# Query columns of the first layer in seven products, sixteen convolution taps and the channel norm moved into attention

## The chip, the core and the metric

One core of one Trainium2 chip runs the whole program in fp32. The metric is the device time of one execution in microseconds, lower is better.

## What is computed

Two layers of a diffusion backbone on 256 context and 256 latent tokens (T = 512, D = 1024). Cut to what matters here, a layer is:

```python
h = rms_norm(x) * (1 + scale) + shift                       # modulated by c
cq, ckv, kr, glu, dq, dk, dv, gates = split(h @ w_in)       # one projection, three branches
a, g = split(glu); u = a * sigmoid(g)                       # 512 channels
u = depthwise_conv(u, conv_w, 31 taps) + conv_b             # along the tokens
o_conv = silu(layer_norm(u, ln_g, ln_b))                    # norm over the 512 channels
o_mla  = attend(q, k, v)                                    # 8 heads, from cq, ckv, kr
o_diff = diff_attend(dq, dk, dv, lam)                       # 4 heads of two maps each
y = sum(sigmoid(gates[b]) * (o_b @ w_o_b) for b in branches)
x = x + g1 * (y @ w_out)
x = x + g2 * moe(rms_norm(x) * ...)                         # 32 experts, two per token
```

Context tokens share all weights and attend to context alone. The second layer keeps only the latent tokens. `dq`, `dk` and `dv` are 512 columns wide.

## The kernel before

The program is written by hand for five engines: TensorE (PE), ACT, DVE, POOL and SP, which only issues DMAs. Each engine has its own function with the instructions in the order in which they run; they meet at semaphores. Weights come in units of up to 2 MB through a ring of three slots (`ring`, loaded by SP in a fixed order: glu0, lora, glu1, dq, ukv, dk, dv, mg0, mg1, mo0, ...). PE's `mm` (L474) writes PSUM banks of two classes: "a" banks are evicted by ACT (through the helper `f`, L1358) and "d" banks by DVE. Every fp32 matmul leaves two records in the trace.

*Projections.* PE computes the GLU columns, the low-rank columns, then `dq`, `ukv` (with `uq`), `dk`, `dv`. `dq` is four output tiles of 128 columns, eight matmuls of 512 tokens each; ACT copies a tile to `qd` and writes its latent half once more with swapped blocks, for the rotary part (`swapped` tells DVE). `dk` and `dv` are already computed in Strassen's form (Winograd's variant): instead of eight products of quarters there are seven, named q, x, r, 11, 12, y, z, each four matmuls of 256 tokens. It needs sums of quarters of the weights, made on DVE: s1 and s2 before the products (`key_sums_ahead`), s4 and s3 in place of weights that the products q and x have read (`key_sums_behind`), sums of quarters of the tokens (`h_sums`), and additions of the results (`key_tiles`).

*Convolution.* The 31 taps of four channel tiles are 124 instructions on DVE, each 128x512: a `scalar_tensor_tensor` through the helper `stt` (L1865) that adds a weighted shift of the input. `conv(n)` writes the next n of them; DVE spreads them between its other work in the projections. When the last is done DVE sets `conv_v`.

*Attention and merge.* Layer 0 then has 32 units (8 heads in blocks) and the units of the differential branch behind them. In unit u PE does `turn(u)` (four or two transposes of probabilities, L857, which wait for `pt_ready` of the unit before and for the probabilities of this one), `scores(u+2)`, the values of the unit before, and some matmuls of the merge (the gate columns, `group_step`, again in seven products, with weight sums on POOL: `sums_ahead`, `sums_behind`; then the branch columns, `branch_step`). DVE does `peak(u+2)` (row maxima, L2288), `probs(u+1)` (L2302, L2303), copies of the values (L2317) and additions of merge tiles (L2411 to L2425). ACT copies the transposed probabilities (`pt_copy(u)`, which sets `pt_ready`) and computes the exponentials.

*Channel norm.* A table of unit numbers says in which unit each step of the norm stands, the same table for all engines (`conv_norm(u)` in each): LN_MEAN (POOL adds the channel tiles, PE sums over the partitions, DVE subtracts the mean, four `stt`), squares on ACT a unit later, LN_VAR (again POOL and PE), CONV_ROOT (reciprocals on DVE), CONV_SCALE (DVE), CONV_TANH (ACT), CONV_OUT (DVE, four `stt` that set `conv_out`).

*What follows `conv_out` in layer 0.* SP loads 1 MB of rows (`silu_load`, L3168, "crow") into the region where the norm kept its squares and its sigmoids, so it waits for all four `conv_out`. ACT has one instruction on these rows, `silu_tanh`, 128x2048, written behind the exponential of unit 22; in ACT's queue the `pt_copy` of unit 23 stands behind it. DVE multiplies the rows in unit 24 and SP loads the first columns of the next modulation after that.

Of the kernel before, what the change touches and what calls it, by code (L numbers as in the profile page):

```python
# [9 lines left out]
KD = D // 128  # L10
# [63 lines left out]
def build(nc, a):  # L74
# [15 lines left out]
    with ctx:  # L90
# [22 lines left out]
        yt = [arena[:, 16384 + T * c:16384 + T * c + T] for c in range(4)] + [yt_more[:, c] for c in range(3)] + [arena[:, 43760:44272]]  # L113
# [165 lines left out]
        AHEAD_SUMS = [("tokens", 0)] + [(w_, "dk") for w_ in ("s1", "s2", "s4_0", "s3_0", "s4_1", "s3_1")] + [(w_, "dv") for w_ in ("s1", "s2", "s4", "s3")]  # L279
        STEPS = [(*w_, 0) for w_ in AHEAD_SUMS] + [("s1", 0, 0), ("s2", 0, 0)]  # L280
# [5 lines left out]
        STEPS += [(*w_, 1) for w_ in AHEAD_SUMS]  # L286
# [151 lines left out]
        def _(pe):  # L438
# [197 lines left out]
            for l in range(DEPTH):  # L636
# [58 lines left out]
                w = grid(unit(("dq", l, 0))[:, 0:4096], KD)  # L695
                for i in range(HD):
                    column_tile("a", ("dq", l, i), lambda k: w[:, k, 128 * i:128 * i + 128], q0, 128, KD, h)
                    if i == 0:
                        ada_finish(("glu", l, 1))
                used(("dq", l, 0), "a")  # L700
                ada_units(("dq", l, 0))
# [16 lines left out]
                w = unit(("dk", l, 0))[:, 0:4096].rearrange("p (k g t m) -> p k g t m", k=KD, g=2, t=2)  # L718
                key_sum = arena[:, 26864:27888].rearrange("p (k g m) -> p k g m", k=4, g=2)
                pe.wait_ge(sums_ready, pool_sums("tokens", 0, l))  # L720
                for g in range(2):
                    w11, w12, w21, w22 = w[:, 0:4, g, 0], w[:, 4:8, g, 0], w[:, 0:4, g, 1], w[:, 4:8, g, 1]
                    for name, cls, cols, toks, needs in (("q", "a", w11, h[:, 0:4, 0:CTX], None), ("x", "a", w21, h_sums[0], "s1"),
                                                         ("r", "d", key_sum[:, :, g], h_sums[1], "s2"), ("11", "d", w12, h[:, 4:8, 0:CTX], None),
                                                         ("12", "d", w11, h[:, 4:8, CTX:T], f"s4_{g}"), ("y", "d", w21, h_sums[2], f"s3_{g}"),
                                                         ("z", "d", w22, h_sums[3], None)):
                        ps = begin(cls, (name, l, "dk", g))
                        if needs:
                            pe.wait_ge(sums_ready, pool_sums(needs, "dk", l))
                        for k in range(4):  # L730
                            last = mm(ps[:, 0:CTX], cols[:, k, :], toks[:, k, :], k == 0, k == 3)
                        end(cls, last)
                used(("dk", l, 0), "d")
                ada_units(("dk", l, 0))
# [618 lines left out]
        def _(act):  # L1353
# [97 lines left out]
            for l in range(DEPTH):  # L1451
# [65 lines left out]
                for i in range(HD):  # L1517
                    ps = take(("dq", l, i))
                    f(qd[:, i, q0:T], ps[:, 0:NQ], ACT.Copy)
                    ins = swap_blocks(PTq[:, i, :], ps[:, CTX - q0:NQ])  # L1520
                    give(ins)
# [1967 lines left out]
```

## Time and profile before

| | |
|---|---|
| three runs, us | 1452.44, 1456.43, 1459.77 (median 1456.43) |
| the profiled execution, us | 1456.56 |
| its span, first to last instruction, us | 1454.6 |
| busy: PE, DVE, ACT, POOL | 1371.5, 802.9, 400.4, 151.6 us |
| mean granted clock of PE | 0.983 of full |

PE is busy for 94% of the span. The 40 slices of the page show DVE at 8 to 9 tenths in the projections (up to about 208 us) and at less in the first attention; POOL is used there for the weight sums. The chain of work that ended last is PE for 74%, with waits for expert weights and for DVE in the later stages. Layer 0's projections run from about 47 to 208 us, its attention from 208 to about 414 us.

### The profile page before, as it was taken

What the parts mean: (1) busy time and instruction counts of PE and PEld (TensorE: products, weight loads), DVE (VectorE), ACT (ScalarE), POOL (GpSimd) and SP (SyncE); (2) the same over time, 40 slices, a digit from 0 to 9 for tenths busy, and PEclk for the clock granted to TensorE, in tenths of its full rate; (3) what the DMA queues carried; (4) which work ended last, traced back from release to release, by engine and by line L of the source; (5) the groups of instructions that cost most, each with busy time, mean ns of one, the idle gap of its engine ahead of it and who ended that gap; (6) DMA issues with size and microseconds to landing.
All of it is one profiled execution on the core that took longest, in us unless ns stands there. A gap on an engine that the chain in (4) does not pass through costs nothing.

```text
span 1454.6 us, 20103 instructions
## 1 busy us (share of the span) xinstructions
PE 1371.5 (94%) x7782; PEld 855.9 (59%) x7782; DVE 802.9 (55%) x1830; ACT 400.4 (28%) x883; POOL 151.6 (10%) x126
## 2 busy tenths in 40 slices
PE   5999999999999999989998869999999999999876
PEld 3444777754444445655555437777678876666543
DVE  2499875778897944523131117996853434344322
ACT  4113634532222012312221224363442203000001
POOL 0020033200011210012212110101000110000000
PEclk9999999999999999989999999999999999999998
DMA  9412230144526446399999968234523489999996
GB/s 379 171 36 79 95 116 11 77 147 171 181 80 227 192 189 274 131 354 418 419 419 420 415 259 342 94 116 144 185 77 145 177 325 378 399 419 420 419 420 239
DMA packets 59553, 347.69 MB, mean 239 GB/s; under 512 B 8388, under 2 KB 15172, under 8 KB 28352
## 3 DMA queue, kind: packets, MB, share of 16 engines
q1 hardware_dynamic: 53856, 335.86, 58.5%
q0 software_dynamic: 5024, 8.40, 1.6%
q10 hardware_dynamic: 576, 2.10, 0.4%
q8 instruction: 65, 1.06, 0.3%
q14 instruction: 32, 0.26, 0.1%
HBM read 343.44 MB, written 11.80 MB: 244 GB/s over the span
## 4 chain that ended last, share of the span: by engine, by line
PE 74%; DVE 8%; SPq 8%; DMA 7%; issue 1%; ACT 1%; DVEq 0%; POOLq 0%; ACTq 0%
PE bank L474 70%; DMA arena<-w_up_in 5%; SPq L3246 4%; DVE arena L1865 4%; SPq L3212 2%; PE bank L857 2%; SPq L3260 2%; DMA arena<-y 1%; PE bank L1232 1%; PE bank L574 1%; ACT arena L1358 1%; DMA x<-x_in 1%; DVE am L2288 0%; PE bank L1252 0%; DVE arena L2393 0%
## 5 line engine op out<-in xcount | busy, mean ns | idle before, releaser
L474 PE MATMUL bank<-arena 128*128 128x256 f32 (+9 forms) x5848 | 1125.7, 428 | 23.9 <-DMA arena<-w_up_in 12.8
L474 PEld LDWEIGHTS bank<-arena 128*128 128x128 f32 (+3 forms) x5848 | 644.3, 161 | 425.4 <-issue 311.4
L1358 ACT ACTIVATE arena<-bank 128x512 f32<-128x512 f32 (+5 forms) x439 | 202.7, 481 | 818.9 <-PE bank L474 718.8
L1865 DVE SCALAR_TENSOR_TENSOR arena<-arena,bank 64x256 f32<-64x256 f32 (+2 forms) x121 | 57.7, 478 | 242.7 <-ACT arena L1358 183.6
L1865 DVE SCALAR_TENSOR_TENSOR arena<-arena,early 128x512 f32<-128x512 f32 (+1 forms) x254 | 138.7, 612 | 0.9
L2288 DVE TENSOR_REDUCE am<-bank 128x1 f32<-128x512 f32 (+1 forms) x96 | 55.4, 598 | 73.9 <-PE bank L474 73.6
L1358 ACT ACTIVATE arena<-bank,am 128x512 f32<-128x512 f32 (+1 forms) x96 | 58.6, 613 | 115.2 <-DVE am L2291 115.0
L3030 POOL TENSOR_TENSOR arena<-arena 128x512 f32<-128x512 f32 (+1 forms) x32 | 37.3, 1167 | 369.4 <-DVE arena L1865 369.4
L1358 ACT ACTIVATE arena<-arena 32x256 f32<-32x256 f32 (+5 forms) x99 | 48.2, 516 | 15.3 <-DVE arena L2317 9.9
L3069 POOL DMA_INDIRECT y<-arena,routing x33 | 32.9, 997 | 180.7 <-ACT arena L1358 180.7
L474 PE MATMUL bank<-down_last,arena 128*128 128x256 f32 (+2 forms) x192 | 46.8, 469 | 1.0 <-DVE arena L2723 0.6
L857 PEld LDWEIGHTS bank<-con,arena 128*128 128x128 f32 x240 | 29.9, 141 | 25.4 <-issue 12.3
L857 PE MATMUL bank<-con,arena 128*128 128x128 f32 x240 | 38.6, 275 | 4.6 <-DVE arena L2303 4.6
L474 PE MATMUL bank<-down_more,arena 128*128 128x256 f32 (+2 forms) x160 | 41.1, 510 | 1.0 <-DVE arena L2723 1.0
L2390 DVE SCALAR_TENSOR_TENSOR arena<-arena 128x1024 f32<-128x1024 f32 x28 | 34.1, 1217 | 5.9 <-DMA arena<-adaT_in 5.9
L474 PEld LDWEIGHTS bank<-down_last,arena 128*128 128x128 f32 (+2 forms) x192 | 28.2, 170 | 10.4 <-issue 6.2
L2393 DVE SCALAR_TENSOR_TENSOR arena<-arena 128x1024 f32<-128x1024 f32 x28 | 34.1, 1219 | 0.0
L474 PE MATMUL bank<-con 128*128 128x128 f32 x178 | 24.4, 292 | 10.0 <-DVE x L1948 10.0
L1358 ACT ACTIVATE arena<-x 128x1024 f32<-128x1024 f32 x14 | 14.8, 1056 | 67.8 <-DVE x L2552 47.0
L574 PE MATMUL bank<-con,arena 128*128 128x128 f32 x112 | 16.5, 299 | 16.2 <-ACT arena L1358 16.2
L2550 DVE TENSOR_TENSOR arena<-bank,arena 128x512 f32<-128x512 f32 x12 | 8.3, 692 | 40.0 <-PE bank L474 40.0
L2860 DVE COPY arena<-bank 128x128 f32<-128x128 f32 x33 | 9.6, 291 | 36.6 <-PE bank L1252 36.2
(262 smaller groups left out, 992.9 us busy)
## 6 DMA issues: line engine op xcount, KB each, us to landing
arena<-w_gate_in SPq DMA_DIRECT2D x60, 1024.0 KB, 22.1
arena<-w_up_in SPq DMA_DIRECT2D x60, 1024.0 KB, 24.4
arena<-w_down_in SPq DMA_DIRECT2D x45, 1024.0 KB, 20.7
arena<-mg_in SPq DMA_DIRECT2D x12, 2048.0 KB, 8.1
arena<-adaT_in SPq DMA_DIRECT2D x40, 512.0 KB, 3.6
arena<-adaT_in SPq DMA_DIRECT2D x16, 1024.0 KB, 7.0
arena<-ada_in SPq DMA_DIRECT2D x6, 2048.0 KB, 15.7
arena<-mo_in SPq DMA_DIRECT2D x6, 2048.0 KB, 8.4
```

The source lines that it names most:

```text
L474: return nc.tensor.matmul(out, w, rhs, start=start, stop=stop)
L574: last = nc.tensor.transpose(ps[:, 128 * k:128 * k + 128], src[:, 512 * half + 128 * k:512 * half + 128 * k + 128], ident)
L857: last = nc.tensor.transpose(PS[6][:, kt * 128:kt * 128 + 128], src[:, kt * 128:kt * 128 + 128], ident)
L1358: return nc.scalar.activation(out, in_, fn, **kw)
L1865: return V.scalar_tensor_tensor(out, in0, sc, in1, op0=op0, op1=op1)
L2288: ins = V.reduce_max(am[:, c + m:c + m + 1], PS[b][:, 0:nk], AX.X)
L2390: V.scalar_tensor_tensor(column_product, w, 1.0, grid(silu_at[l][:, 0, :], m), op0=MUL, op1=MUL, accum_out=ada[l][:, c_, 0:1]).then_inc(dv ...
L2393: V.scalar_tensor_tensor(w, w, 1.0, grid(silu_at[l][:, 1 - l, :], m), op0=MUL, op1=MUL, accum_out=ada[l][:, c_, 1 - l:2 - l]).then_inc(dve ...
L3030: G.tensor_tensor(yt[c][:, q0:T], yt[c][:, q0:T], gt8[:, c, q0:T], op=ADD).then_inc(s[done], 1)
L3069: pool.indirect_dma_start(out=yd[l][:, :], out_offset=bass.IndirectOffsetOnAxis(ap=to, axis=0), in_=yy[0:64 + C, p, :], in_offset=None, bo ...
L3212: sp.dma_start(to[..., 512 * q:512 * q + 512], src[..., 512 * q:512 * q + 512]) \
L3246: sp.dma_start(to, src).then_inc(gu_ready[j], 16)
```

## The change

Four things, cut to their core.

1. In layer 0 `dq` is computed in the seven products too: 14 products of four matmuls of 256 tokens in place of 4 x 8 matmuls of 512. The code of `dk` becomes `paired_columns(of)` and serves both. DVE gets the weight sums and result sums of `dq`; ACT copies q and x and writes the swapped blocks from SBUF when a group of tiles is complete.
2. Sixteen taps of layer 0 (two in each of units 0 to 7) leave the projections for attention, and the norm's steps stand later.
3. The merge's intermediate tiles `yt` change places, so that the tiles written first don't lie on the input of the late taps; POOL adds the norm's channels later in its order.
4. In layer 1 some taps change places with the key additions, one or two positions.

```diff
-        yt = [arena[:, 16384 + T * c:16384 + T * c + T] for c in range(4)] + [yt_more[:, c] for c in range(3)] + [arena[:, 43760:44272]]
+        yt = [yt_more[:, c] for c in range(3)] + [arena[:, 43760:44272]] + [arena[:, 16384 + T * c:16384 + T * c + T] for c in range(4)]
...
+        PAIRED = (("dq", "dk"), ("dk",))
...
-        LN_MEAN, LN_VAR = (3, 2), (8, 7)
-        CONV_ROOT = ({9 + c: (c,) for c in FOUR}, {8: (0,)})
-        CONV_SCALE = ({13 + c: (c,) for c in FOUR}, {8: FOUR})
-        CONV_TANH = ({15 + c: (c,) for c in FOUR}, {10: FOUR})
-        CONV_OUT = ({17 + c: (c,) for c in FOUR}, {12: FOUR})
+        LATE_TAPS = (2,) * 8
+        LN_MEAN, LN_VAR = (10, 2), (14, 7)
+        CONV_ROOT = ({15: (0, 1), 16: (2, 3)}, {8: (0,)})
+        CONV_SCALE = ({17: (0, 1), 18: (2, 3)}, {8: FOUR})
+        CONV_TANH = ({19: (0, 1), 20: (2, 3)}, {10: FOUR})
+        CONV_OUT = ({21: (0, 1), 22: (2, 3)}, {12: FOUR})
...
+                if l == 0:
+                    paired_columns("dq")
+                    ada_finish(("glu", l, 1))
+                else:
...
+                if l == 0:
+                    for g in range(2):
+                        ps = take(("q", l, "dq", g))
+                        give(f(qd[:, 2 * g, 0:CTX], ps[:, 0:CTX], ACT.Copy))
+                        ps = take(("x", l, "dq", g))
+                        give(f(qd[:, 2 * g + 1, CTX:T], ps[:, 0:CTX], ACT.Copy))
+                    for g in range(2):
+                        act.wait_ge(empty["d"], Dn[("z", l, "dq", g)])
+                        for i in (2 * g, 2 * g + 1):
+                            ins = swap_blocks(PTq[:, i, :], qd[:, i, CTX:T])
+                    ins.then_inc(s["swapped"], 1)
...
-                    if b == 0 and c == 0:
+                    if b == 0 and c == 4:
                         act.wait_ge(s["conv_v"], seen(l, "conv_v", 1))
...
                 conv(12)
+                if l == 0:
+                    pair_sums_ahead("dq")
                 glu_up(3)
...
-                conv(16)
+                if l == 0:
+                    conv(4)
+                    pair_sums_behind("dq", 0)
+                else:
+                    conv(16)
...
+                if l == 0:
+                    pair_tiles("dq", 0, 2)
+                    pair_tiles("dq", 0, 3)
+                    pair_sums_behind("dq", 1)
...
-                conv(len(CONV) - conv_at[0])
...
+                conv(len(CONV) - conv_at[0] - (0 if l else sum(LATE_TAPS)))
...
                 def conv_norm(u):
...
+                    if l == 0 and u < len(LATE_TAPS):
+                        conv(LATE_TAPS[u])
+                        if u == len(LATE_TAPS) - 1:
+                            conv_end()
...
                     sums_behind(0, 0)
                     upper(0, 0)
                     sums_ahead(0, 1)
                     corner(0, 0)
+                    sums_behind(0, 1)
+                    upper(0, 1)
+                    sums_ahead(0, 2)
+                pool.wait_ge(s["conv_v"], seen(l, "conv_v", 1))
+                pool.wait_ge(full["a"], A[("uv", l, 3)])
+                add_channels(cv)
+                if l == 0:
+                    corner(0, 1)
                 pool.wait_ge(s["conv_sq"], seen(l, "conv_sq", CT))
                 add_channels(lora)
```

What the tables of units do to the order is plainer in the order itself. First DVE at the `dq` columns; the last GLU tile is the row whose input is `arena,bank`. Before:

```order
L1865 SCALAR_TENSOR_TENSOR arena<-arena,early 128x512 [waits dve_step] x12
L1865 SCALAR_TENSOR_TENSOR arena<-arena,bank 128x2x256 [waits act_tile_empty,dve_tile_full]
L1865 SCALAR_TENSOR_TENSOR arena<-arena,early 128x512 [waits dve_step,dve_tile_empty]
L1865 SCALAR_TENSOR_TENSOR arena<-arena,early 128x512 [waits dve_step] x3
L2037 TENSOR_SCALAR arena<-arena,early 128x512 x2
L1865 SCALAR_TENSOR_TENSOR arena<-arena,early 128x512 [waits dve_step] x10
L2094 RECIPROCAL arena<-arena 128x512 [waits act_tile_empty]
```

and with the change:

```order
L1889 SCALAR_TENSOR_TENSOR arena<-arena,early 128x512 [waits dve_step] x12
L2162 TENSOR_TENSOR arena<-arena 128x8x128 [waits ring_ready0]
L2163 TENSOR_TENSOR arena<-arena 128x1024 [waits sums_ready]
L1889 SCALAR_TENSOR_TENSOR arena<-arena,bank 128x2x256 [waits act_tile_empty,dve_tile_full,sums_ready]
L1889 SCALAR_TENSOR_TENSOR arena<-arena,early 128x512 [waits dve_step,dve_tile_empty]
L1889 SCALAR_TENSOR_TENSOR arena<-arena,early 128x512 [waits dve_step] x3
L2169 TENSOR_TENSOR arena<-arena 128x4x128 [waits act_tile_full]
L2171 TENSOR_TENSOR arena<-arena 128x4x128 [waits act_tile_full,sums_ready]
L2219 RECIPROCAL arena<-arena 128x512 [waits act_tile_empty,sums_ready]
```

The two sums ahead stand in front of the last GLU tile, and two sums behind stand where twelve taps and bias instructions were.

Next DVE in units 19 to 24, at the last steps of the channel norm; the `stt` that waits `conv_act` is CONV_OUT, the one of 128x2048 is DVE's part on the rows. Before, from unit 19 on:

```order
L1865 SCALAR_TENSOR_TENSOR arena<-arena 128x512 [waits conv_act]
L2288 TENSOR_REDUCE am<-bank 128x1 [waits scores]
L2291 TENSOR_SCALAR am<-am 128x1 [waits dve_step]
L2302 RECIPROCAL am<-am 128x1 [waits exp_ready_0]
L2303 TENSOR_SCALAR arena<-arena,am 128x512 [waits dve_step]
L2317 COPY arena<-bank 128x128 [waits pv_full]
L2411 TENSOR_TENSOR arena<-arena,bank 128x256 [waits act_tile_empty,dve_tile_full]
L1865 SCALAR_TENSOR_TENSOR arena<-arena 128x512 [waits conv_act]
```

and with the change, from the end of unit 21 to the end of unit 22:

```order
L2475 TENSOR_TENSOR arena<-arena,bank 128x256 [waits sums_ready,dve_tile_full]
L1889 SCALAR_TENSOR_TENSOR arena<-arena 128x512 [waits conv_act] x2
L2345 TENSOR_REDUCE am<-bank 128x1 [waits scores]
L2348 TENSOR_SCALAR am<-am 128x1 [waits dve_step]
L2359 RECIPROCAL am<-am 128x1 [waits exp_ready_0]
L2360 TENSOR_SCALAR arena<-arena,am 128x512 [waits dve_step]
L2374 COPY arena<-bank 128x128 [waits pv_full]
L2478 TENSOR_TENSOR arena<-bank,arena 128x256 [waits dve_tile_full]
L1889 SCALAR_TENSOR_TENSOR arena<-arena 128x512 [waits conv_act] x2
```

The last CONV_OUT stood behind the merge tile L2411 in unit 20; now it stands behind the merge tile of L2478 (L2421 before) in unit 22.

Last ACT from the late tanh steps (`arena<-arena,early`) to the rows. With the change:

```order
L1370 ACTIVATE arena<-arena,early 128x512 [waits conv_scaled]
L1370 ACTIVATE arena<-arena 128x512 [waits conv_act]
L1370 ACTIVATE arena<-bank 128x512 [waits pt_full]
L1370 ACTIVATE arena,am<-bank,am 128x512 [waits pt_full,scores_max]
L1370 ACTIVATE arena<-bank 128x512 [waits pv_full,pt_full]
L1370 ACTIVATE arena,am<-bank,am 128x256 [waits pt_full,scores_max]
L1370 ACTIVATE arena<-arena 128x2048 [waits silu_rows_loaded]
L1370 ACTIVATE arena<-bank 128x512 [waits pt_full]
L1370 ACTIVATE arena,am<-bank,am 128x256 [waits pt_full,scores_max]
```

Here the rows' instruction (128x2048) keeps its place behind the exponential of unit 22 and ahead of the copy of unit 23; the norm's steps have moved towards it.

## Rows read from the trace of the kernel before

**Rows 1.** The page: busy time of the engines, share of the span, instructions.

```profile
PE 1371.5 (94%) x7782; PEld 855.9 (59%) x7782; DVE 802.9 (55%) x1830; ACT 400.4 (28%) x883; POOL 151.6 (10%) x126
```

**Rows 2.** Windows: length, busy PE, PEld, DVE, ACT, POOL, clock, DMA share, GB/s.

```profile
114.00:141.00 27.00, 27.00 (x64) 11.98 (x63) 26.69 (x35) 8.38 (x18) 0.00 (x0) 1.00 0.15 64
208.00:250.00 42.00, 40.43 (x216) 30.72 (x218) 21.54 (x65) 19.62 (x47) 16.57 (x15) 1.00 0.14 51
```

**Rows 3.** Timeline of ACT: start, us, instructions, idle before and releaser in brackets.

```profile
121.29 2.14 ACT L1358 ACTIVATE arena<-bank 128x512 f32<-128x512 f32 x5 [5.18 <-PE bank L474]
128.09 2.14 ACT L1358 ACTIVATE arena<-bank 128x512 f32<-128x512 f32 x5 [4.67 <-PE bank L474]
...
160.78 0.38 ACT L1358 ACTIVATE arena<-bank 128x256 f32<-128x256 f32 x1 [0.85 <-PE bank L474]
162.51 0.39 ACT L1358 ACTIVATE arena<-bank 128x256 f32<-128x256 f32 x1 [1.34 <-PE bank L474]
```

**Rows 4.** Timeline of DVE in the projections.

```profile
111.47 0.69 DVE L1865 SCALAR_TENSOR_TENSOR arena<-arena,bank 128x512 f32<-128x512 f32 x1 [4.71 <-PE bank L474]
...
115.77 6.71 DVE L1865 SCALAR_TENSOR_TENSOR arena<-arena,early 128x512 f32<-128x512 f32 x10
...
133.09 1.23 DVE L2191 TENSOR_TENSOR arena<-arena 128x1024 f32<-128x1024 f32 x1
...
160.78 0.69 DVE L2198 TENSOR_TENSOR arena<-arena 128x512 f32<-128x512 f32 x1 [1.02 <-PE bank L474]
...
164.24 0.42 DVE L2127 TENSOR_TENSOR arena<-arena,bank 128x256 f32<-128x256 f32 x1 [0.18 <-PE bank L474]
```

**Rows 5.** Timelines of PE (two turns), DVE (mean) and ACT (squares) in attention.

```profile
252.28 0.38 PE L857 MATMUL bank<-con,arena 128*128 128x128 f32 x2
...
255.15 0.66 PE L857 MATMUL bank<-con,arena 128*128 128x128 f32 x4
...
224.91 2.48 DVE L1865 SCALAR_TENSOR_TENSOR arena<-bank,arena 128x512 f32<-128x512 f32 x4 [0.82 <-PE bank L474]
...
228.89 2.18 ACT L1358 ACTIVATE arena<-arena 128x512 f32<-128x512 f32 x4
```

**Rows 6.** Timelines of DVE, SP, ACT, PE around the rows' load, and its DMA issue.

```profile
285.56 0.69 DVE L1865 SCALAR_TENSOR_TENSOR arena<-arena 128x512 f32<-128x512 f32 x1
...
293.43 0.42 DVE L2421 TENSOR_TENSOR arena<-bank,arena 128x256 f32<-128x256 f32 x1 [1.54 <-PE bank L474]
...
286.27 0.33 SPq L3168 DMA_DIRECT2D arena<-crow_in  x1
...
arena<-crow_in SPq DMA_DIRECT2D x1, 1024.0 KB, 4.6
...
292.52 1.91 ACT L1358 ACTIVATE arena<-arena 128x2048 f32<-128x2048 f32 x1
294.32 0.59 ACT L1358 ACTIVATE arena<-bank 128x512 f32<-128x512 f32 x1
...
295.83 0.38 PE L857 MATMUL bank<-con,arena 128*128 128x128 f32 x2
```

**Rows 7.** Timeline of PE and windows (columns of Rows 2) where the clock was down.

```profile
780.17 6.59 PE L474 MATMUL bank<-arena 128*64 128x256 f32 x32 [1.57 <-DMA arena<-w_up_in]
...
831.90 3.67 PE L474 MATMUL bank<-arena 128*64 128x256 f32 x32
...
873.91 3.78 PE L474 MATMUL bank<-con 128*128 128x128 f32 x16 [10.04 <-DVE x L1948]
...
873.00:874.50 1.50, 0.59 (x3) 0.59 (x3) 1.47 (x2) 0.55 (x1) 0.00 (x0) 0.50 0.97 415
877.50:879.00 1.50, 1.50 (x10) 1.24 (x10) 1.21 (x4) 1.14 (x2) 0.00 (x0) 0.74 1.05 448
```

**Rows 8.** Timelines of DVE and POOL: one `stt` while POOL adds.

```profile
278.04 1.45 DVE L1865 SCALAR_TENSOR_TENSOR arena<-arena 128x512 f32<-128x512 f32 x1
...
277.85 1.09 POOL L2988 TENSOR_TENSOR arena<-arena,routing 128x512 f32<-128x512 f32 x1 [4.35 <-PE bank L474]
```

More of the change, by code:

```diff
@@ L693, in _ @@
                 sums(("loraS", l, 0), [P[:, 0, q0:T]])
[L695 to L701, printed above, removed]
+                key_sum = arena[:, 26864:27888].rearrange("p (k g m) -> p k g m", k=4, g=2)
@@ new lines, in paired_columns @@
+                def paired_columns(of):
+                    w = unit((of, l, 0))[:, 0:4096].rearrange("p (k g t m) -> p k g t m", k=KD, g=2, t=2)
+                    pe.wait_ge(sums_ready, pool_sums("tokens", 0, l))
+                    for g in range(2):
+                        w11, w12, w21, w22 = w[:, 0:4, g, 0], w[:, 4:8, g, 0], w[:, 0:4, g, 1], w[:, 4:8, g, 1]
+                        for name, cls, cols, toks, needs in (("q", "a", w11, h[:, 0:4, 0:CTX], None), ("x", "a", w21, h_sums[0], "s1"),
+                                                             ("r", "d", key_sum[:, :, g], h_sums[1], "s2"), ("11", "d", w12, h[:, 4:8, 0:CTX], None),
+                                                             ("12", "d", w11, h[:, 4:8, CTX:T], f"s4_{g}"), ("y", "d", w21, h_sums[2], f"s3_{g}"),
+                                                             ("z", "d", w22, h_sums[3], None)):
+                            ps = begin(cls, (name, l, of, g))
+                            if needs:
+                                pe.wait_ge(sums_ready, pool_sums(needs, of, l))
+                            for k in range(4):
+                                last = mm(ps[:, 0:CTX], cols[:, k, :], toks[:, k, :], k == 0, k == 3)
+                            end(cls, last)
+                    used((of, l, 0), "d")
+                    ada_units((of, l, 0))
@@ new lines, in _ @@
+                if l == 0:
+                    paired_columns("dq")
+                    ada_finish(("glu", l, 1))
+                else:
+                    w = grid(unit(("dq", l, 0))[:, 0:4096], KD)
+                    for i in range(HD):
+                        column_tile("a", ("dq", l, i), lambda k: w[:, k, 128 * i:128 * i + 128], q0, 128, KD, h)
+                        if i == 0:
+                            ada_finish(("glu", l, 1))
+                    used(("dq", l, 0), "a")
+                    ada_units(("dq", l, 0))
@@ L716, in _ @@
                 ada_units(("ukv", l, 0))
[L718 to L734, printed above, removed]
+                paired_columns("dk")
                 w = grid(unit(("dv", l, 0))[:, 0:4096], KD)
@@ L1516, in _ @@
                 act.wait_ge(empty["d"], Dn[("gluA", l, CT - 1)])
[L1517 to L1521, printed above, removed]
-                act.wait_ge(empty["a"], A[("dq", l, HD - 1)])
-                act.sem_inc(s["swapped"], 1)
+                if l == 0:
[4 more added lines that the diff above has]
+                        give(f(qd[:, 2 * g + 1, CTX:T], ps[:, 0:CTX], ACT.Copy))
+                    for g in range(2):
+                        act.wait_ge(empty["d"], Dn[("z", l, "dq", g)])
[3 more added lines that the diff above has]
+                else:
+                    for i in range(HD):
+                        ps = take(("dq", l, i))
+                        f(qd[:, i, q0:T], ps[:, 0:NQ], ACT.Copy)
+                        ins = swap_blocks(PTq[:, i, :], ps[:, CTX - q0:NQ])
+                        give(ins)
+                    act.wait_ge(empty["a"], A[("dq", l, HD - 1)])
+                    act.sem_inc(s["swapped"], 1)
                 ada_raw(("dq", l, 0))
@@ L3019, in _ @@
                 if l == 0:
-                    for n in range(1, N_GROUPS):
+                    for n in range(2, N_GROUPS):
                         sums_behind(n // 4, n % 4)
```

189 lines of the change are left out of this document (102 added, 87 removed).

## Prediction

> **What bounds the kernel now.** I read the page first, then the windows of layer 0, then single engines in order of time. PE is busy for 94% of the span [rows 1], and in the two stretches that the change touches it is closer still: 27.00 of 27 us at the `dq` columns and 40.43 of 42 us in the first ten units of attention, both at the full granted clock, 2.4 GHz [rows 2]. There a microsecond of PE work saved is a microsecond of time, and a microsecond in which PE waits for another engine is one lost. DVE is nearly as full at `dq` (26.69 of 27) but has room in attention (21.54 of 42) [rows 2]; ACT has more. So the question is what PE saves at `dq`, and whether the work moved into attention ever stands on the path that releases PE. That path passes once per unit: probabilities on DVE, the turn on PE, the copy of the turned tile on ACT, the next turn.
>
> **The `dq` columns: a saving.** Two tiles reach ACT 6.80 us apart [rows 3]; the four take 27.5 us by the evictions of all of them (6.80 to 6.87 apart). A product of `dk`, with four matmuls of 256 tokens, takes 162.51 - 160.78 = 1.73 us [rows 3]. Fourteen make 24.2. PE saves 3.3 us.
>
> DVE must keep up. Removed there before attention are 16 taps at 6.71/10 = 0.67, 10.7 us [rows 4]. Added are two sums of 128x1024 at 1.23, four of 128x512 at 0.69 and fourteen result additions of 128x256 at 0.42 to 0.45, together 11.5 us [rows 4]. The sums ahead (2.5 us) stand before the last GLU tile, where DVE was idle for 4.71 us [rows 4], so they cost nothing. Set in order behind that tile, s4 and s3 of the first group come about 4 us, those of the second about 1.5 us before PE wants them (my estimate from these durations, the two reciprocals in between included). The 0.8 us net lies on taps that nobody waits for. ACT's swapped copies now start only when a group is complete, and end about 2 us behind the last product; I take 0.25 us of wait for PE at the following `uq` tiles, between 0 and 1. So attention starts 3.05 us earlier; bounds -3.3 (nothing lost) and 0 (sums late by what the products save).
>
> **The late taps in units 0 to 7: nothing.** Two taps are 1.35 us, the sixteen 10.7. DVE idles for 42 - 21.54 = 20.5 us of the ten units, about 2 us in each [rows 2], mostly in front of the row maxima, where a tap delays nothing that PE has made yet. A tap may run slower beside POOL: one 128x512 `stt` took 1.45 us while POOL added, where the same took 0.69 alone [rows 6, 8]. POOL is busy for 16.57 of the 42 us [rows 2], so of 16 taps some 39% are hit, 16 x 0.39 x 0.76 = 4.7 us more of DVE, where 20.5 - 10.7 = 9.8 us of idle time are left. From rows I take 0, with 4.7 as the upper end. The Trainium skill (GPSIMD Engine Reference, Specifications) says that GpSimd shares its SBUF interfaces with VectorE and contends with instructions that read two SBUF inputs, which a tap does: by that rule the move into the stretch where POOL makes weight sums is bad, and the sum would be up to 4.7 us longer than with taps at their price alone.
>
> POOL itself now adds the channels twice behind the sums of groups 1 and 2. Its next sums have a few microseconds to spare by my order of POOL's work, so I take 0.
>
> **The mean and the squares, units 10 to 12: 1.5 us.** Four subtractions took 2.48 us [rows 5] and stand ahead of the maxima and probabilities that the next turn waits for. The unit that gets them is short: two turns are 255.15 - 252.28 = 2.87 us apart [rows 5]. With about 1.4 us for maxima and probabilities, 2.48 + 1.4 ends some 1.15 us behind the turn. Four squares on ACT, 2.18 us [rows 5], stand ahead of the next copy and cost 0.3 to 0.4 more. Bounds: 0 (hidden in full) and 2.5 (the mean in full).
>
> **The rows behind `conv_out`: 6.4 us.** This is the step that decides. Before, the last CONV_OUT ends at 285.56 + 0.69 = 286.25, and SP issues the 1 MB load at 286.27. It lands 4.6 us later, at 290.9. ACT reaches the instruction on these rows at 292.52, 1.6 us after the landing, so nothing waits [rows 6]. With the change the last two CONV_OUT stand behind the merge tile that starts at 293.43, in unit 22: 293.43 + 0.34 + 2 x 0.69 = 295.15. This tile waits for PE, so it can't come earlier against PE's work. The load is issued at 295.2 and lands at 299.8. ACT's place in its order has not moved: it arrives at 292.5 and waits. The instruction holds ACT for 294.32 - 292.52 = 1.80 us, to 301.6; the copy of unit 23 behind it takes 0.59, to 302.2 [rows 6]. PE's turn of unit 24, at 295.83 before [rows 6], needs that copy. PE has nothing else in its order and waits 302.2 - 295.83 = 6.4 us. Bounds 5.4 (landing 1 us faster) and 8 (the load meets that of the next merge weights, which SP issues just behind it).
>
> **The clock after that wait: 2.6 us.** After 10.04 us of idle PE's granted clock was at half, 1.2 GHz, when it restarted at 873.91 (0.50), and it was on its way up at 877.5 (0.74 in that window) [rows 7]. A wait of 1.57 us, behind a thin stretch of small matmuls, was followed by 6.59 us for 32 records that took 3.67 at full clock: 2.92 us lost [rows 7]. Sixteen records of 128x128 took 3.78 us at half clock, some 1.9 more than at full. I take 2.6, between 0 (no fall) and 3.1. The 1.15 us of unit 12, in the middle of dense work, I give nothing.
>
> **The rest.** What follows is released by PE or by weights loaded in PE's wake, so the shift passes to the end. The few taps that change places in layer 1 keep the sums there ahead of PE: nothing. The new homes of `yt` are addresses alone.
>
> **The sum.** -3.05 + 0 + 1.5 + 6.4 + 2.6 = +7.45 us. Against the profiled execution, 1456.56, that is 1464.0. It lies 0.13 us above the median of the runs shown, which changes nothing; those runs spread from 1452.4 to 1459.8. Half a per cent, about what a measurement of this kernel tells from no change, is 7.3 us: 1463.7 is the line, and the forecast lies on it.
>
> **The rivals.**
>
> *The clock holds, or falls for less.* For it: in attention PE is at full work up to the wait, and no row shows 6 us of idle in such a stretch. Against it: the two rows above. The sum without the clock is +4.85, 1461.4. Chance 0.14.
>
> *The rows come in time (not slower).* One mechanism: ACT meets the rows already landed. It would need the last CONV_OUT done by about 288.8: the copy has to end by 295.8, the tanh by 295.2, so the rows must be there by 293.4, less 4.6. That is 6.4 us earlier than I place it, in unit 20 or 21 instead of 22. For it: DVE has idle time around there. Against it: the order of DVE puts the last pair behind the merge tile of unit 22, which PE releases. Then -3.05 + 1.5 = -1.55 is left, 1455.0, and with the mean hidden too 1453.5. Chance 0.07.
>
> *DVE falls behind in units 0 to 7.* Taps slowed by POOL push the probabilities past the turns, up to 4.7 us on top: 1464.0 + 4.7 = 1468.7. For it: the 1.45 us [rows 8], and units that differ in length. Against it: DVE idles for half of the stretch [rows 2]. It decides where both taps of a unit are slowed and the unit is a short one. Chance 0.11.
>
> *The saving isn't there.* The products of `dq` wait for their weight sums, because DVE is full in that stretch, and attention starts when it did: 1464.0 + 3.05 = 1467.1. Against it: 1.5 us of slack by my order. Chance 0.06.
>
> **How the numbers follow.** The forecast has 0.62; its own range is 1461 to 1467, about half on each side of 1463.7: 0.31 slower and 0.31 same. The clock's rival adds 0.14 to same. The rows in time give 0.04 to same and 0.03 to faster. The last two give 0.17 to slower. Faster 0.03, same 0.49, slower 0.48. The range goes from 1457 to 1470: it leaves out the rows in time and the far ends of the bounds, and takes in the others.
>
> **What would show it.** In the changed profile the last product of `dq` should be evicted about 3 us earlier than the last tile was, and PE should show no wait for DVE there. The load of the rows should be issued behind two `stt` at the merge tile of unit 22, ACT should be idle 6 to 7 us with that DMA as releaser, and PE should have one wait of 6.4 us before a turn, released by ACT, with a granted clock near half for some microseconds after it. A short wait of about 1 us on DVE should stand at unit 12. I am wrong if no wait over 3 us stands on PE between units 20 and 26, or if the larger loss lies in units 0 to 8.

## The result and the profile after

| | before | with the change |
|---|---|---|
| median of 7 runs each, us | 1454.97 | 1461.23 |
| lowest to highest | 1452.18 to 1459.77 | 1458.7 to 1464.7 |
| profiled execution, its span | 1456.56, 1454.6 | 1462.23, 1460.3 |

The ratio is 1.0043, 95% interval 1.0024 to 1.0063: slower by 6.3 us in the medians. Measured once more, beside three of the experiments, it was 1463.54 to 1454.21 (6 and 16 runs), ratio 1.0067, interval 1.0045 to 1.0088. The forecast was 1464.0 in a range of 1457 to 1470.

The page of the changed kernel, its line of engines and its group of turns (lines have moved: L474 is L477 now, L857 is L869, L1358 is L1370, L1865 is L1889, L2421 is L2478):

```profile
PE 1370.4 (94%) x7830; PEld 865.8 (59%) x7830; DVE 814.0 (56%) x1850; ACT 399.7 (27%) x883; POOL 153.7 (11%) x126
...
L869 PE MATMUL bank<-con,arena 128*128 128x128 f32 x240 | 38.8, 276 | 11.4 <-ACT arena L1370 6.8
```

and the same group before:

```profile
L857 PE MATMUL bank<-con,arena 128*128 128x128 f32 x240 | 38.6, 275 | 4.6 <-DVE arena L2303 4.6
```

PE is busy for 1.1 us less than before [rows 1] and the program is longer: what was lost is for the most part idle time. The turns (L869) have 11.4 us of it in front of them, where it was 4.6, and 6.8 of the 11.4 are released by ACT.

**Where the time went.** PE runs the same instructions in both programs almost everywhere, so the same instruction can be looked up in both timelines. Three pairs show the projections. Before:

```profile
111.36 1.04 PE L474 MATMUL bank<-arena,con 128*32 128x512 f32 x2
...
208.26 2.83 PE L474 MATMUL bank<-arena 96*128 96x256 f32 x12 [0.90 <-issue]
...
301.14 0.38 PE L857 MATMUL bank<-con,arena 128*128 128x128 f32 x2
```

and with the change, PE's timeline through attention, with its longest waits in brackets (a wait of 1.17 us for DVE in unit 1 is left out, since the kernel before has it too):

```profile
110.97 1.04 PE L477 MATMUL bank<-arena,con 128*32 128x512 f32 x2
...
204.59 2.83 PE L477 MATMUL bank<-arena 96*128 96x256 f32 x12 [0.90 <-issue]
...
246.85 1.10 PE L477 MATMUL bank<-arena,ones 128*128 128x512 f32 x2 [0.17 <-DVE arena L2482]
247.78 0.38 PE L869 MATMUL bank<-con,arena 128*128 128x128 f32 x2
...
252.39 0.70 PE L477 MATMUL bank<-down_more,arena 128*128 128x256 f32 x2 [2.07 <-ACT arena L1370]
...
267.40 1.13 PE L477 MATMUL bank<-down_last,arena 128*128 128x256 f32 x4 [0.63 <-DVE arena L2475]
...
301.84 0.66 PE L869 MATMUL bank<-con,arena 128*128 128x128 f32 x2 [6.37 <-ACT arena L1370]
302.29 6.64 PE L477 MATMUL bank<-arena 96*128 96x256 f32 x26
308.77 0.38 PE L869 MATMUL bank<-con,arena 128*128 128x128 f32 x2
```

An instruction just ahead of the query columns comes 0.39 us earlier than before (the start of a program moves by -1.1 to +1.0 us between the profiles of this case), the first of attention 3.67 earlier: the seven products save 3.28 us. The turn of unit 24 comes 6.01 later than before [rows 6], the next one, 301.14 to 308.77, 7.63 later. From there the shift stays at 7.6 for the rest of layer 0's attention and for all that follows up to 620 us, where the experts begin.

The chain behind the wait of 6.37 us, on DVE, SP and ACT:

```profile
292.91 0.42 DVE L2478 TENSOR_TENSOR arena<-bank,arena 128x256 f32<-128x256 f32 x1 [0.88 <-PE bank L477]
293.25 1.82 DVE L1889 SCALAR_TENSOR_TENSOR arena<-arena 128x512 f32<-128x512 f32 x2
...
295.10 0.33 SPq L3230 DMA_DIRECT2D arena<-crow_in  x1
...
299.30 1.91 ACT L1370 ACTIVATE arena<-arena 128x2048 f32<-128x2048 f32 x1 [7.19 <-DMA arena<-crow_in]
301.12 0.58 ACT L1370 ACTIVATE arena<-bank 128x512 f32<-128x512 f32 x1
```

The last pair of CONV_OUT ends at 295.07, the load is issued at 295.10, ACT starts on the rows at 299.30 after 7.19 us of idle time released by this DMA, the copy of unit 23 ends at 301.70 and PE's turn starts at 301.84. It is [rows 6] once more, with the load 8.83 us later.

The windows around it (columns of [rows 2]) show the clock:

```profile
295.50:298.00 2.50, 0.00 (x0) 0.00 (x0) 0.84 (x4) 0.00 (x0) 0.00 (x0) 1.00 0.79 324
298.00:301.80 3.80, 0.00 (x0) 0.00 (x0) 0.00 (x0) 2.50 (x3) 0.00 (x0) 0.56 1.01 412
301.80:303.30 1.50, 1.46 (x6) 0.84 (x6) 0.00 (x0) 0.35 (x2) 0.00 (x0) 0.50 1.15 492
303.30:304.80 1.50, 1.50 (x15) 1.50 (x16) 1.34 (x5) 0.00 (x0) 0.00 (x0) 0.50 0.06 22
304.80:306.30 1.50, 1.50 (x9) 0.69 (x6) 1.50 (x1) 0.94 (x4) 0.00 (x0) 0.83 0.00 0
```

It fell in the idle time, was at 0.50 (1.2 GHz) when PE went on, and rose within 304.8 to 306.3. Between the turns of units 24 and 25 lie 6.93 us; before they were 301.14 - 295.83 = 5.31. That is 1.62 us.

The wait of 2.07 us at 252.39 is the mean's. DVE and ACT in front of it:

```profile
247.98 2.48 DVE L1889 SCALAR_TENSOR_TENSOR arena<-bank,arena 128x512 f32<-128x512 f32 x4 [1.28 <-PE bank L477]
250.38 0.68 DVE L2345 TENSOR_REDUCE am<-bank 128x1 f32<-128x512 f32 x1
...
251.28 0.69 ACT L1370 ACTIVATE arena<-bank,am 128x512 f32<-128x512 f32 x1 [2.70 <-DVE am L2348]
...
251.96 0.38 ACT L1370 ACTIVATE arena<-bank 128x256 f32<-128x256 f32 x1
```

The four subtractions, 2.48 us, delay the row maximum; ACT's exponential waits 2.70 us for it; and behind that exponential, in ACT's order, stands the copy at 251.96 that empties a PSUM bank for PE's next merge product. It is the bank that PE waits for, not the turn.

In the later stages the shift wanders: it is between 4.6 and 8.2 us in the first of those with expert weights and 6.00 in layer 1's projections, where PE waits for a weight sum. Before, and with the change:

```profile
966.24 1.97 PE L474 MATMUL bank<-arena 128*128 128x256 f32 x8 [1.03 <-DVE arena L2198]
```

```profile
973.18 2.64 PE L477 MATMUL bank<-arena 128*128 128x256 f32 x8 [1.96 <-DVE arena L2169]
```

Behind this wait the shift is 8.63; the clock fell here too. It isn't a steady cost of the taps that change places in layer 1: in the other ten profiles with those places the wait is 0.98 to 1.94 us and the shift moves by -0.04 to +0.92 there. At the end of the span 5.7 us are left.

### The profile page after: what moved, and what is told of

Read it like the earlier page. It is cut to its first block, busy times and chain, and to the rows that moved or that the text cites. A ratio compares the mean times of both kernels' runs of the same rounds, so it can differ in the third digit from the quotient of the medians.

```text
span 1460.3 us, 20236 instructions
## 1 busy us (share of the span) xinstructions
PE 1370.4 (94%) x7830; PEld 865.8 (59%) x7830; DVE 814.0 (56%) x1850; ACT 399.7 (27%) x883; POOL 153.7 (11%) x126
## 4 chain that ended last, share of the span: by engine, by line
PE 75%; DVE 9%; DMA 9%; SPq 3%; issue 2%; ACT 1%; DVEq 0%; POOLq 0%; ACTq 0%
PE bank L477 70%; DMA arena<-w_up_in 7%; DVE arena L1889 4%; SPq L3274 2%; PE bank L869 2%; DMA arena<-y 1%; ACT arena L1370 1%; PE bank L1244 1%; SPq L3308 1%; PE bank L577 1%; DVE am L2345 0%; DMA x<-x_in 0%; PE bank L1264 0%; DMA arena<-crow_in 0%; DVE arena L2326 0%
## 5 line engine op out<-in xcount | busy, mean ns | idle before, releaser
L477 PE MATMUL bank<-arena 128*128 128x512 f32 (+9 forms) x5832 | 1108.7, 425 | 24.7 <-DMA arena<-w_up_in 13.2
L477 PEld LDWEIGHTS bank<-arena 128*128 128x128 f32 (+4 forms) x5832 | 641.3, 160 | 412.1 <-issue 296.5
L1370 ACT ACTIVATE arena<-bank 128x256 f32<-128x256 f32 (+4 forms) x423 | 195.9, 483 | 816.6 <-PE bank L477 710.6
L1889 DVE SCALAR_TENSOR_TENSOR arena<-arena,bank 64x256 f32<-64x256 f32 (+2 forms) x121 | 57.7, 479 | 243.7 <-ACT arena L1370 183.8
L1889 DVE SCALAR_TENSOR_TENSOR arena<-arena,early 128x512 f32<-128x512 f32 (+1 forms) x254 | 142.0, 623 | 0.9
L1370 ACT ACTIVATE arena<-bank,am 128x512 f32<-128x512 f32 (+1 forms) x96 | 58.6, 613 | 113.6 <-DVE am L2348 113.4
L1370 ACT ACTIVATE arena<-arena 32x256 f32<-32x256 f32 (+5 forms) x115 | 54.7, 502 | 29.5 <-DVE arena L2374 9.9
L477 PE MATMUL bank<-down_last,arena 128*128 128x256 f32 (+2 forms) x224 | 55.5, 465 | 1.6 <-DVE arena L2475 0.6
L477 PE MATMUL bank<-down_more,arena 128*128 128x256 f32 (+2 forms) x192 | 48.1, 484 | 3.1 <-ACT arena L1370 2.1
L869 PE MATMUL bank<-con,arena 128*128 128x128 f32 x240 | 38.8, 276 | 11.4 <-ACT arena L1370 6.8
L869 PEld LDWEIGHTS bank<-con,arena 128*128 128x128 f32 x240 | 29.9, 141 | 32.5 <-issue 19.7
L477 PEld LDWEIGHTS bank<-down_last,arena 128*128 128x128 f32 (+2 forms) x224 | 35.0, 177 | 13.1 <-issue 6.5
L477 PEld LDWEIGHTS bank<-down_more,arena 128*128 128x128 f32 (+2 forms) x192 | 27.9, 170 | 11.7 <-issue 6.1
L477 PE MATMUL bank<-con 128*128 128x128 f32 x178 | 25.0, 297 | 9.7 <-DVE x L1972 9.7
L1370 ACT ACTIVATE arena<-x 128x1024 f32<-128x1024 f32 x14 | 14.8, 1055 | 66.7 <-DVE x L2609 47.0
```

What stands on the lines that cost most here:

```text
L477: return nc.tensor.matmul(out, w, rhs, start=start, stop=stop)
L869: last = nc.tensor.transpose(PS[6][:, kt * 128:kt * 128 + 128], src[:, kt * 128:kt * 128 + 128], ident)
L1370: return nc.scalar.activation(out, in_, fn, **kw)
L1889: return V.scalar_tensor_tensor(out, in0, sc, in1, op0=op0, op1=op1)
```

## The experiments

Each row is PE's timeline of one profile, as the shift in us of the same instruction against the kernel before (the 111.36, 208.26, 252.28, 295.83 and 301.14 us rows, and one at 419.81; the last transposes of layer 0's attention stand at 445.6). The first column is the start's own movement; the others are read against it. By the turn of unit 11 the kernels with the late norm gain some 0.8 us, and the two with the mean in unit 11 some 2.1, because one or both of PE's sums for the norm (245.02 to 245.88 is one, before) then stand behind it. Medians and ratios stand with the experiments.

| | ahead of dq | attention starts | turn of unit 11 | of unit 24 | of unit 25 | late in attention |
|---|---|---|---|---|---|---|
| the change | -0.39 | -3.67 | -4.50 | +6.01 | +7.63 | +7.64 |
| the change again | +0.95 | -2.33 | -3.16 | +8.05 | +9.54 | +9.55 |
| rows a unit later | +0.01 | -3.29 | -4.11 | +2.50 | +2.99 | +3.17 |
| norm earlier | +0.71 | -2.58 | -3.41 | +2.88 | +2.88 | +2.89 |
| filled wait | +0.35 | -2.93 | -3.76 | +7.03 | +7.05 | +7.06 |
| filled wait again | +0.71 | -2.57 | -3.40 | +7.53 | +7.55 | +7.56 |
| plain dq | -0.58 | -0.58 | -1.41 | +11.49 | +13.48 | +13.49 |
| norm late alone | +0.12 | +0.12 | -0.71 | +10.13 | +11.71 | +11.71 |
| three edits | -0.54 | -3.83 | -5.92 | -0.63 | +0.44 | +0.60 |
| edits, norm spread | -0.61 | -3.89 | -5.99 | -1.49 | -1.49 | -1.49 |
| dq alone | -1.13 | +5.59 | +5.60 | +5.60 | +5.60 | +5.61 |

**The rows' instruction a unit later.** The theory is that the rows stand at the root. ACT only:

```diff
-                    if columns[0] and l == 0 and u == COLUMN_FROM[0] - 3:
+                    if columns[0] and l == 0 and u == COLUMN_FROM[0] - 2:
                         silu_tanh()
```

> Theory (the loss is PE's wait for ACT, which waits for the rows): ACT's instruction on the rows now stands behind the exponential of unit 23, not 22, so the copy of unit 23 is free. The wait of 6.4 us at the turn of unit 24 goes; one of about 1 us is left a unit later, since the rows land at about 299.3 and the copy then ends at 301.7. No long idle, so the clock stays up: 1461.2 - 5.3 - 1.6 = 1454.3. Rival (the late taps slowed beside POOL are the loss): nothing changes in units 0 to 8, 1461.

Measured: 1456.8 (12 runs) against 1455.09, ratio 1.0009, interval 0.9993 to 1.0024. The wait is gone; ACT still waits for the rows, a unit later, where PE loses 0.28:

```profile
298.33 0.44 PE L869 MATMUL bank<-con,arena 128*128 128x128 f32 x2 [0.63 <-DVE arena L2360]
...
304.13 0.41 PE L869 MATMUL bank<-con,arena 128*128 128x128 f32 x2 [0.28 <-ACT arena L1370]
...
301.81 1.91 ACT L1370 ACTIVATE arena<-arena 128x2048 f32<-128x2048 f32 x1 [3.40 <-DMA arena<-crow_in]
```

The median is 4.4 us lower where 6.9 were expected. In this profile some 1.8 us are lost elsewhere: behind the mean's wait of 2.07 us, which both kernels have, the clock fell here and not in the profile of the change. Without it the table would show 6.7 us saved. Windows of this kernel, then the one of the change that answers to the second:

```profile
252.70:254.20 1.50, 1.43 (x7) 1.07 (x8) 0.00 (x0) 1.50 (x5) 0.00 (x0) 0.90 0.46 197
254.20:255.70 1.50, 1.50 (x4) 0.26 (x4) 0.15 (x1) 1.50 (x4) 0.00 (x0) 0.50 0.00 0
```

```profile
254.20:255.70 1.50, 1.50 (x13) 1.14 (x13) 1.21 (x4) 1.50 (x4) 0.18 (x1) 1.00 0.00 0
```

**The norm's end earlier**, so that the load is issued in time instead of awaited later:

```diff
-        CONV_SCALE = ({17: (0, 1), 18: (2, 3)}, {8: FOUR})
-        CONV_TANH = ({19: (0, 1), 20: (2, 3)}, {10: FOUR})
-        CONV_OUT = ({21: (0, 1), 22: (2, 3)}, {12: FOUR})
+        CONV_SCALE = ({16: (0, 1), 17: (2, 3)}, {8: FOUR})
+        CONV_TANH = ({17: (0, 1), 18: (2, 3)}, {10: FOUR})
+        CONV_OUT = ({19: (0, 1), 20: (2, 3)}, {12: FOUR})
```

> Theory (rows wait): scale, tanh and CONV_OUT stand one to two units earlier, the last CONV_OUT in unit 20 as before, so the rows land before ACT comes to them. The wait and the clock's loss behind it both go: 1461.2 - 6.4 - 1.6 = 1453.2, some 2 below the kernel before. The mean's wait of some 2 us at unit 11 stays. Rival (late taps): 1461.

Measured: 1457.18 (12 runs) against 1455.09, ratio 1.0017, interval 1.0005 to 1.0029. No wait at unit 24, and between the turns of units 24 and 25 nothing is lost. But two waits are new, one behind two reciprocals and two scalings in a row on DVE (3.4 us from 272.74 on), the other behind ACT's four instructions for the tanh of two channels (281.92 to 284.58):

```profile
277.15 0.44 PE L869 MATMUL bank<-con,arena 128*128 128x128 f32 x2 [1.12 <-DVE arena L2360]
...
285.00 0.63 PE L869 MATMUL bank<-con,arena 128*128 128x128 f32 x4 [1.23 <-ACT arena L1370]
```

Both experiments take the wait away, one at the consumer and one at the producer, so the rows are its cause. Neither wins back all that was expected: the first loses to the clock behind another wait, the second because steps pressed together cost waits of their own.

**The wait filled.** 25 matmuls that compute nothing, in front of the turn of unit 24, in a bank that is free there:

```diff
                 for u in range(len(AU)):
+                    if l == 0 and u == 24:
+                        pe.wait_ge(s["exp_ready"], 23)
+                        keep_busy(PS[4], 25)
                     turn(u, P[:, u % 4], AU[u][2])
```

> 25 extra matmuls of 128x128 stand in front of the turn of unit 24 and fill most of PE's wait; the turn still starts when ACT's copy is done. Theory (the 1.6 us between this turn and the next are the lowered clock): they go, 1459.6. Rival (they are work that piled up on ACT and DVE in the wait): 1461.2 as with the change.

> The filled wait once more, beside the kernel with the change in the same call, since its trace showed the two turns 1.3 us closer and its time did not. Theory (the lowered clock costs 1.6 behind the wait of unit 24, and later stages spread the times): 1 to 2 us under after_again. Rival (the extra matmuls make something later slower): 2 us or more above after_again.

```profile
296.05 5.74 PE L477 MATMUL bank<-con 128*128 128x128 f32 x50
302.86 0.41 PE L869 MATMUL bank<-con,arena 128*128 128x128 f32 x2 [1.06 <-ACT arena L1373]
303.10 5.25 PE L477 MATMUL bank<-arena 96*128 96x256 f32 x26
308.19 0.38 PE L869 MATMUL bank<-con,arena 128*128 128x128 f32 x2
...
303.50:305.00 1.50, 1.50 (x18) 1.15 (x18) 1.19 (x5) 0.17 (x1) 0.00 (x0) 1.00 0.59 251
```

With PE at work the granted clock stays at 1.00, the 26 records behind the turn take 5.25 us instead of 6.64, and the two turns are 5.33 us apart. In both profiles the table shows 0.02 us between units 24 and 25 where the change loses 1.5 to 1.6. So those 1.6 us are the lowered clock. The medians do not show it: 1464.44 (6 runs) against 1455.09, and again 1463.94 beside 1463.54 of the change. The profiled executions, 1461.03 and 1461.8, are 1.2 and 1.8 us shorter than the two of the change, but they are among the fastest of their six. That the filled wait makes the program faster is not shown.

**The change once more.**

> The kernel with the change once more, beside the runs of this call: the median between 1459 and 1463. In some executions the granted clock may fall behind the 2.07 us wait of unit 11 too, as it did in two of the four runs so far (1.6 us more), in some not.

1463.54 (6 runs), 0.5 above the band that was expected. The wait of unit 24 is 7.07 us here: from the issue of the load to ACT's start on the rows it took 4.90 us, in the first profile 4.20.

**Plain query columns again**, everything else as in the change: the products of `dq`, its sums on DVE and the copies from SBUF are taken out, `LATE_TAPS` stays:

```diff
-        PAIRED = (("dq", "dk"), ("dk",))
+        PAIRED = (("dk",), ("dk",))
...
-                if l == 0:
-                    paired_columns("dq")
-                    ada_finish(("glu", l, 1))
-                else:
+                if True:
                     w = grid(unit(("dq", l, 0))[:, 0:4096], KD)
...
```

> The query columns of layer 0 in plain form again, late taps and norm as in the change. Theory (the seven products save their 3.3 us in full): attention starts 3.3 us later, everything after it as with the change: 1464.5. Rival (the saving comes back as a wait for DVE before attention): within 1 us of 1461.2.

Measured: 1468.79 (6 runs), ratio 1.0091, interval 1.007 to 1.0112. Attention starts exactly when it did before (-0.58, as ahead of dq). So the saving of 3.3 us is whole: no wait for DVE eats it. The time is 4 above the expectation. In the profile attention costs 2.8 us more than with the change: some 1.8 are the clock behind the 2.07 us wait, which fell here too, since the same records take 2.50 and 2.26 us instead of 1.61 and 1.56; the rest is a longer wait at unit 24 (6.92) and the clock behind it:

```profile
255.48 0.70 PE L477 MATMUL bank<-down_more,arena 128*128 128x256 f32 x2 [2.07 <-ACT arena L1367]
...
256.45 2.50 PE L477 MATMUL bank<-arena 96*128 96x512 f32 x10
258.89 2.26 PE L477 MATMUL bank<-down_more,arena 128*128 128x256 f32 x6
```

**The norm late alone**: plain query columns as in the experiment before, and all taps in the projections.

```diff
-        LATE_TAPS = (2,) * 8
+        LATE_TAPS = (0,) * 8
```

> Plain query columns, no taps in attention, only the norm at its later units. Theory (late taps cost nothing, the norm's place costs it all): PE's waits of 2 us at unit 11 and 6.4 at unit 24 stay, and it takes as long as with plain query columns and late taps, 1468.8 within 2; attention starts within 0.5 us of the kernel before. Rival (taps slowed beside POOL): up to 4.7 us less, 1464, and units 0 to 8 shorter by that.

Measured: 1467.13 (6 runs) against 1454.21, ratio 1.0091, interval 1.0072 to 1.011. Without one tap in attention it is as slow as with sixteen, within the 2 us that were expected. From the start of attention to the turn of unit 11 the shift moves by -0.83 with the taps and without them: they cost nothing there. The late norm alone costs the 11.6 us of its row (11.71 less the start's 0.12). With the taps it was 14.1; the 2.5 between the two are the clock behind the 2.07 us wait, which did not fall here, and the shorter wait (6.69) and stretch of low clock at unit 24. POOL's new order, which belongs to the late norm here, was not tried by itself; in the profile of the change no wait of PE in this attention is released by POOL.

**Three edits together.**

```diff
-        LN_MEAN, LN_VAR = (10, 2), (14, 7)
+        LN_MEAN, LN_VAR = (11, 2), (14, 7)
...
-                    if columns[0] and l == 0 and u == COLUMN_FROM[0] - 3:
+                    if columns[0] and l == 0 and u == COLUMN_FROM[0] - 2:
...
                     corner(0, 1)
+                    sums_behind(0, 2)
                 pool.wait_ge(s["conv_sq"], seen(l, "conv_sq", CT))
...
```

> The whole change with three edits: the rows' instruction on ACT one unit later, the mean one unit later (unit 11, in front of a longer unit), POOL's second channel sum behind the weight sums of group 2. Theory: the wait of unit 24 falls to about 0.9 in all, the one of unit 11 from 2.07 to about 0.3 at unit 13, no fall of the clock: 1461.2 - 5.5 - 1.6 - 1.8 - 0.8 = 1451.5, under the kernel before (1455.1) by 3.6. Rival (the mean's wait only moves along): 1453.5 to 1454.

Measured: 1455.71 (12 runs) against 1454.21, ratio 1.0004, interval 0.9989 to 1.002. The rival was nearer, and both were too low: in the table attention ends 1.1 us later against its start than before. The mean's wait shrank and moved, 0.42 and 1.07 us in place of 2.07 and 0.17, and two short waits are left around units 24 and 25:

```profile
249.75 1.10 PE L477 MATMUL bank<-arena,ones 128*128 128x512 f32 x2 [0.42 <-ACT arena L1370]
...
255.30 0.70 PE L477 MATMUL bank<-down_more,routing 128*128 128x256 f32 x2 [1.07 <-ACT arena L1370]
...
295.20 0.44 PE L869 MATMUL bank<-con,arena 128*128 128x128 f32 x2 [0.63 <-DVE arena L2360]
...
301.58 0.41 PE L869 MATMUL bank<-con,arena 128*128 128x128 f32 x2 [0.85 <-ACT arena L1370]
```

**The same with the norm's end spread:**

```diff
-        CONV_TANH = ({19: (0, 1), 20: (2, 3)}, {10: FOUR})
-        CONV_OUT = ({21: (0, 1), 22: (2, 3)}, {12: FOUR})
+        CONV_TANH = ({18: (0,), 19: (1, 2), 20: (3,)}, {10: FOUR})
+        CONV_OUT = ({19: (0,), 20: (1, 2), 21: (3,)}, {12: FOUR})
```

> The combination with the mean and the rows' instruction one unit later, and the norm's end spread: tanh one, two, one channels in units 18 to 20, CONV_OUT in 19 to 21. Theory (what is left of the loss are short waits that late work on DVE and ACT makes): the wait of 0.63 at the turn of unit 24 and of 0.85 at the next go, 1.07 at unit 12 and 0.63 at unit 15 stay: some 1.3 less than the combination, 1454.4. Rival (the waits only move to the units with two tanh): 1455.7 as the combination.

Measured: 1451.99 (12 runs) against 1457.16 (23 runs), ratio 0.9974, interval 0.9958 to 0.999: faster than the kernel before, and below both expectations. Both waits are gone. The load is issued at 289.17 and ACT takes the rows at 294.15 without waiting:

```profile
289.17 0.33 SPq L3232 DMA_DIRECT2D arena<-crow_in  x1
...
294.15 1.91 ACT L1370 ACTIVATE arena<-arena 128x2048 f32<-128x2048 f32 x1
```

In the table its attention ends 0.9 us earlier against its own start than before, and 2.0 earlier than with the three edits alone. By the interval the gain over the kernel before is 1.5 to 6.1 us. Only those 0.9 are found in layer 0's attention; where the rest comes from is open, and the kernel before, measured beside this experiment on another chip, was 2 to 3 us slower than beside the others (1454.2 to 1455.1).

**Seven products alone**: no late taps, the sixteen taps left among the others in the projections, POOL's order and the norm's as in the kernel before.

```diff
-        LATE_TAPS = (2,) * 8
-        LN_MEAN, LN_VAR = (10, 2), (14, 7)
+        LATE_TAPS = (0,) * 8
+        LN_MEAN, LN_VAR = (3, 2), (8, 7)
...
+        CONV_OUT = ({17 + c: (c,) for c in FOUR}, {12: FOUR})
...
```

> Seven products for the query columns, but all taps in the projections and the norm and POOL in the order of the kernel before. Theory (DVE is full there, its idle time between the query columns and attention is some 5 us in the trace with the change, the taps are 10.7): PE waits 5 to 9 us for the weight sums of the value columns, so attention starts 2 to 6 us later than before instead of 3.3 earlier, and in attention nothing is lost: 1457 to 1461. Rival (DVE has room enough): 1452.

Measured: 1458.89 (10 runs) against 1457.16, ratio 1.0023, interval 1.0006 to 1.004. Attention starts 6.7 us later than before (5.59, and the start's own 1.13), above the 2 to 6 expected. PE waits once, for a weight sum of the value columns that stands behind nineteen taps in DVE's order, and behind this wait the clock was at half:

```profile
188.97 3.62 PE L477 MATMUL bank<-arena 128*128 128x256 f32 x16
199.58 6.47 PE L477 MATMUL bank<-arena 128*128 128x256 f32 x16 [6.99 <-DVE arena L2139]
...
201.00:202.50 1.50, 1.50 (x5) 1.23 (x4) 1.47 (x2) 0.00 (x0) 1.50 (x1) 0.50 0.04 11
```

The wait is within the 5 to 9 us expected. The same sixteen records take 2.85 us longer behind it than ahead of it, which the expectation had left out: -3.28 + 6.99 + 2.85 = 6.6. In attention nothing is lost. So in this order of DVE's work the taps do have to leave the projections if PE's saving is to be kept, and units 0 to 7 take them for nothing.

## Why the prediction was right

The time came out inside the range and 2.8 us under the forecast; the mechanism was the one named: the saving at the query columns is there, and it is lost to one wait of PE for a copy that stands behind the rows on ACT. That the sum came so near is in part luck. In the profile the four terms, read as shifts, are -3.28 + 3.15 + 6.53 + 1.62 = 8.02 us against the 7.45 of the forecast; the mean was taken 1.65 too small, the clock 0.98 too large, and from the 8.02 at unit 25 the later stages, which the forecast gave nothing, took some 2 us back. Term by term:

- **Query columns, -3.05.** Measured -3.28 to -3.30 in the eight profiles that have them and the late taps; the fourteen products stand from 113.77 to 137.94, the 24.2 us that were forecast. The quarter of a microsecond that I put on `uq` was not lost; PE shows no wait between the query columns and attention.
- **Late taps, 0.** Right, and shown by leaving them out. Some do run slower while POOL adds: four of the eight pairs took 1.88 to 2.25 us, the others 1.40 or 1.41.

```profile
209.53 1.41 DVE L1889 SCALAR_TENSOR_TENSOR arena<-arena,early 128x512 f32<-128x512 f32 x2
...
211.83 2.25 DVE L1889 SCALAR_TENSOR_TENSOR arena<-arena,early 128x512 f32<-128x512 f32 x2
...
211.92 1.61 POOL L3047 TENSOR_TENSOR arena<-routing,arena 128x512 f32<-128x512 f32 x1 [3.26 <-PE bank L477]
```

The Trainium skill (GPSIMD Engine Reference, Specifications) says that GpSimd's SBUF interfaces are shared with VectorE, with contention for instructions of two SBUF inputs; the trace agrees, with 2.25 us against 1.41. The eight pairs took 2.2 us more of DVE than at 1.41 each, about half of the 4.7 that I had as the upper end, and none of it reached PE: DVE's idle time took it.
- **Mean and squares, 1.5.** Too small: waits of 2.07 + 0.17 at unit 11 and 0.63 at unit 15, and 3.15 in the shift from the start of attention (-3.67) to the row in front of the rows' wait (293.23 before, 292.71 with the change). The step that failed is "ends some 1.15 us behind the turn": I looked for the delay at the turn, and it came through ACT's order, where the copy that frees a bank stands behind the exponential. The wait at unit 15, at the next product behind the variance sum, I had not looked for, and no experiment takes it apart.
- **The rows, 6.4.** The wait is 6.37, by errors that cancel. The last pair of CONV_OUT took 1.82 us, not 1.38 (POOL was adding, 293.42 to 294.53), and from the issue of the load to ACT's start it took 4.20, not 4.6. In three other profiles of kernels with the same place for the norm and the rows (the change again, plain `dq`, the norm late alone) the latter was 4.90, 4.76 and 4.53, and the wait 7.07, 6.92 and 6.69.
- **The clock, 2.6.** 1.62, and 1.5 to 2.0 in those three. I sized it between rows of other stages; the stretch behind this wait is short and the clock came back by about 306.
- **What passes to the end.** I took it that the shift passes whole. It does up to 620 us; 7.64 us late in layer 0's attention became 5.7 in the span. In all eleven profiles the span has 0.5 to 5.3 us less of shift than attention, so part of it may lie in the one profile of the kernel before.

The rival in which the clock holds is excluded by the windows, the one in which DVE falls behind in units 0 to 7 and the one in which the saving is lost by the experiments. The one that ends not slower needed the last CONV_OUT in unit 20 or 21. Two experiments put it there: the rows then come in time in both, but the one with the norm's end earlier alone is still slower than the kernel before (interval 1.0005 to 1.0029), by the mean's wait and two new ones, and only the one with the three edits and the norm spread is faster.

## What to carry to other kernels

When work is moved later to fill idle time, follow what its end releases: here taps that cost nothing made a norm late, the norm's buffer was where a load wanted to land, and the load's reader stood in an in-order queue ahead of a copy that PE needed. An instruction that waits holds everything behind it on its engine, so look at what is queued behind the waiter before pricing the wait, and move either end of it. And where one PE stall is sized, add what the clock costs behind it (here 1.5 to 2.9 us behind waits of 6.4 to 7.1).

## What was not expected of the hardware

The same wait of 2.07 us at the same place was followed by a fall of the granted clock to 0.50 in two of eight profiles (some 1.8 us lost), and by none in the other six. It is the same with a wait of 1.68 us in layer 1's attention, which all twelve profiles have: the clock fell behind it in the kernel before,

```profile
1052.00:1054.00 2.00, 2.00 (x18) 1.58 (x18) 1.40 (x4) 0.04 (x1) 0.00 (x0) 0.59 0.72 227
```

and in the second profile of the filled wait (0.50), where the 26 records behind it took 5.60 us in both, and in none of the other ten, where they took 3.97. What decides between the two is not in these traces. It may be one reason why the medians of these kernels lie up to 4 us from what their waits add up to.
